# A narrower last block in the token-major input projection, and z's first rests moved ahead of a wait

## The chip, the core and the metric

The kernel runs on one core of a Trainium2 chip. The metric is the device time of the whole kernel in microseconds, median over runs; lower is better. The engines are TensorE (PE, with its weight loads PEld), VectorE (DVE), ScalarE (ACT), GpSimd (POOL) and SyncE (SP), which issues the DMAs of the weights.

## What is computed

Two transformer blocks over 256 tokens of width 1024 in f32. The first normalises x and multiplies it with `w_in`; the product is cut into the inputs of sparse attention (q, k, v, the indexer's iq, ik, iw), of a state-space branch (z, xbc, dt) and of the gates. Then come attention, the chunked scan, memory cross attention and a product-key expert layer. The second block is a gated linear recurrence with a convolutional feed-forward part, whose conditions enter by a modulation (`silu(c) @ w_ada`). What matters here is the beginning of the first block, in outline:

```python
IN_SPLIT_SIZES = (1024, 256, 256, 256, 64, 4, 2048, 3072, 32, 2048)  # q k v iq ik iw z xbc dt gate
y = (rmsnorm(x, norm_mix_g) @ w_in).split(IN_SPLIT_SIZES)
y = y * silu(z)                 # later, in the state-space branch
dt = softplus(dt_raw + dt_bias)
```

## The kernel before, in words

Nearly all matmuls are with weights that are streamed once from memory, in tiles of 128 x 1024 f32 (512 KB). SP loads them into `weight_ring`, a ring of four; a slot is loaded again when its tile's rest has been made. Every f32 product is made of three matmuls of the type fp32r: both operands are split into a high part and a rest, and high x high, rest x high and high x rest are accumulated in PSUM. For a weight tile e this goes through three engines, with two buffers each for the parts:

- ScalarE copies the tile to `weight_high` (`split_high`, line 1676 by the helper `func`), once the high matmuls of tile e - 2 are done and its rest is made. Semaphore `hi_ready`.
- VectorE or GpSimd subtracts: `weight_rest = tile - weight_high` (`split_rest`, line 2307 on VectorE, line 851 on GpSimd). It waits for `hi_ready` of the tile and for `hi_begun`, the first high matmul of the tile before. Semaphore `rest_ready`, one counter for both engines, so that the order of the tiles has to be kept.
- TensorE (`split_tile`, lines 964 to 972; matmuls at line 934) does the matmuls with the high part, then waits for `rest_ready` and does those with the rest.

The token-major projections (`split_block`, lines 974 to 999) keep 128 tokens as the stationary operand and stream 512 weight columns. A block is 512 output columns: four weight tiles, each with two chunks of 128 inputs, times two halves of the tokens, so eight high matmuls and four rest matmuls a tile, into two banks. There are four token-major blocks "tok" (tiles 0 to 15: q, k, iq, ik, v, iw, dt), and then four blocks "z" (tiles 16 to 31). The columns of "tok" are 1892, padded with zeros by the host to 2048: the last block holds columns 1536 to 2047, of which 356 carry values. ScalarE copies the banks of each "tok" block into `TOK` (`evacuate_tok`, lines 1761 to 1766), those of block 3 after the high parts of tiles 16 and 17. After that it makes the SiLU of the second block's conditions (`silu_of_conditions`, semaphore `silu_c`), for which it first loads an activation table.

Who makes the rests before the change: tiles 0 to 2 VectorE, 3 to 15 GpSimd (line 855), 16 to 31 VectorE (`z_rests`, line 2393), 32 on GpSimd. VectorE's queue around the change, by hand in this order (lines 2389 to 2425): wait for 16 rests; wait for `silu_c`; `group_sum`, a small reduction; rests of z's tiles 0 and 1; wait for the banks of "tok" and for the rope sines; then the rests of z's tiles 2 to 11 between the rope operations on `TOK` (lines 2415 to 2422); then tiles 12 to 15. Between the rests of z, `add_both` (lines 2370 to 2387) adds four tiles of the modulation's weights, scaled with the SiLU of the conditions, from the same ring; SP's queue waits for each of these sums in its turn, since it loads in the order of the ring.

After z, TensorE waits for `rope_ready` and transposes q, k, iq and ik, does the indexer's products, and then the gate (tiles 32 on, feature-major, 256 columns), the attention and the xbc projection with the convolution on VectorE.

Of the kernel before, what the change touches and what calls it, by code (L numbers as in the profile page):

```python
# [23 lines left out]
TT = T // P  # L24
# [118 lines left out]
for _name, _w in [("ident", P), ("upto", P), ("ones", P), ("after", P), ("before", P), ("causal", P),  # L143
                  ("iota", P), ("freq", 24), ("iota16", 16)]:
    CONST[_name] = (_c, _w)
    _c += _w
N_CONST = _c
N_LEVELS = 7
HALF_LEVELS = (range(0, 4), range(4, 7))
N_MADE = N_LEVELS + 1  # L150
# [305 lines left out]
def build(nc, A):  # L456
    B = plan_banks()
    with ExitStack() as ctx:
# [32 lines left out]
        x1_hi = over("x1_high", "arena", 30208, [P, KC, T])  # L491
        x1_lo = over("x1_rest", "act_feature_major", 0, [P, KC, T])
# [57 lines left out]
        S = {n: sem(n) for n in names}  # L550
# [46 lines left out]
        def claim(name, turn=None):  # L597
            b, n = B.at[name]
            if turn is not None:
                nc.tensor.wait_ge(bank_free[b], turn * B.per[name] + (n - 1))  # L600
            elif n > 1:
                nc.tensor.wait_ge(bank_free[b], n - 1)
            return ps[:, b, :]
# [19 lines left out]
        TOK = area(0, TT, 2048)  # L623
# [142 lines left out]
        tsl = lambda t: slice(t * P, (t + 1) * P)  # L766
# [77 lines left out]
        def _(pool):  # L844
# [7 lines left out]
                                        ALU.subtract).then_inc(S["rest_ready"], 1)  # L852

            pool.wait_ge(S["rest_ready"], 3)
            for e in range(3, 16):
                split_rest(e)
            pool.wait_ge(S["rest_ready"], 32)
            with pool.Fori(0, 2) as i:
# [73 lines left out]
        def _(pe):  # L932
            def mm(out, lhsT, rhs, start=True, stop=True):
                return nc.tensor.matmul(out, lhsT, rhs, start=start, stop=stop, skip_group_check=True)  # L934
# [36 lines left out]
                pe.wait_ge(rest_ready, rest_count)  # L971
                return rest(w_lo[:, e % 2, :])

            def split_block(e, name, b, hi, lo_, parts=None):

                banks = [claim((name, b, t)) for t in range(TT)]
                for j in range(4):
                    if parts is not None:
                        parts(j)

                    def high(w):
                        for t in range(TT):
                            for k in range(2):
                                r = w[:, k * 512:(k + 1) * 512]
                                ins = mm(banks[t], hi[:, 2 * j + k, tsl(t)], r, start=(j == k == 0), stop=False)
                                if t == k == 0:
                                    begun = ins
                                ins = mm(banks[t], lo_[:, 2 * j + k, tsl(t)], r, start=False, stop=False)
                        return begun, ins

                    def rest(w):
                        for t in range(TT):
                            for k in range(2):
                                ins = mm(banks[t], hi[:, 2 * j + k, tsl(t)], w[:, k * 512:(k + 1) * 512],
                                         start=False, stop=(j == 3 and k == 1))
                            if j == 3:
                                filled(ins, (name, b, t))

                    split_tile(e + j, None, 0, high, rest, *rest_count(e + j))
# [39 lines left out]
                    both_ready("x1", 2 + j)  # L1039

            for b in range(4):
                split_block(4 * b, "tok", b, x1_hi, x1_lo, x1_parts if b == 0 else None)
            for b in range(4):
                split_block(E0["in_z"] + 4 * b, "z", b, x1_hi, x1_lo)

# [9 lines left out]
            b = claim(("ad0", "sums"))  # L1055
            for c in range(2):
                for k in range(4):
                    ins = mm(b[:, 2 * k + c:2 * k + c + 1], ADS0[:, c, hsl(k)], C("ones")[:, 0:1])
# [3 lines left out]
            for t in range(TT):  # L1062
                for r in range(2):
                    b = claim(("idx", t, r))
                    rs = slice(r * IDH, (r + 1) * IDH)
                    for c in range(2):
                        ins = mm(b[:, c * T:(c + 1) * T], IQT[rs, c, tsl(t)], IKT[rs, :])
                    filled(ins, ("idx", t, r))
            with pe.Fori(0, 2) as i:
                for j in range(8):  # L1070
                    e = E0["in_gate"] + j
                    split_channels(e, ("gate", j), x1_hi, x1_lo, i, 8, S["rest_ready"], i * 8 + rest_count(e)[1])

            for t in range(TT):
                w = P * (t + 1)
                for p in range(4):
                    b = claim(("lg", t, p))
                    for c in range(2):
                        h = 2 * p + c
                        ins = mm(b[:, c * T:c * T + w], QT[:, h, tsl(t)], KT[:, h // 4, 0:w])  # L1080
# [3 lines left out]
            b = claim(("acs",))  # L1084
# [4 lines left out]
            for x in range(2):  # L1089
                ins = mm(b[64 * x:64 * x + 64, 128:256], ADT.rearrange("p c h -> p (c h)"), C("upto"))  # L1090
# [32 lines left out]
            for n in range(24):  # L1123
                e = E0["in_xbc"] + n
# [85 lines left out]
            for k in range(len(groups) + 1):  # L1210
                if k < len(groups):
                    c, g = groups[k]
                    for half in range(2):
                        b = claim(("row", c, g, half))
# [17 lines left out]
                if k >= 1:  # L1232
# [6 lines left out]
                    b = claim(("yd", c, g))  # L1239
                    for j in range(8):  # L1240
                        h = 8 * g + j
                        ins = mm(b[:, j * SP_:(j + 1) * SP_], EM[:, (k - 1) % 2, j, :],
                                 XS[:, c, h * SP_:(h + 1) * SP_])
                    filled(ins, ("yd", c, g))
                    if c == 0:
                        b = claim(("st", g))
                        filled(mm(b, BTOK[:, g, :], XDTD[:, g * 512:(g + 1) * 512]), ("st", g))
                    else:
                        freed(pe, ("st", g))
                        b = claim(("yo", g))  # L1250
# [3 lines left out]
            for n in range(8):  # L1254
                e = E0["mem_k"] + n
# [9 lines left out]
            for n in range(8):  # L1265
                e = E0["merge"] + 3 * n
# [15 lines left out]
            for n in range(8):  # L1282
                e = E0["cross_q"] + n
# [17 lines left out]
            for t in range(TT):  # L1301
                for p in range(2):
                    b = claim(("cl", t, p))
                    for c in range(2):
                        h = 2 * p + c
                        for k in range(2):
                            ins = mm(b[:, c * T:(c + 1) * T], CQT[:, 2 * h + k, tsl(t)], MKT[:, 2 * h + k, :],
                                     start=(k == 0), stop=(k == 1))
# [15 lines left out]
            for h in range(MH):  # L1324
                b = claim(("co", h))
                for c in range(2):
                    for m in range(TT):
                        ins = mm(b[:, c * T:(c + 1) * T], MV[:, m, h * MD + c * P:h * MD + (c + 1) * P],
                                 CPT[:, m, h, :], start=(m == 0), stop=(m == 1))
# [9 lines left out]
            for t in range(TT):  # L1339
                for h in range(2):  # L1340
                    b = claim(("y", t, h))
# [5 lines left out]
            with pe.Fori(0, 2) as i:  # L1347
                for j in range(8):
                    e = E0["peer_q"] + j
# [4 lines left out]
            for t in range(TT):  # L1354
                for q in range(4):
                    b = claim(("sk", t, q))
# [315 lines left out]
        def _(act):  # L1672
# [5 lines left out]
            def evacuate(job, out, turn=None, f=ACT.Copy, src=None, **kw):  # L1678
                b = arrived(act, job, turn)
                free(func(out, b if src is None else src(b), f, **kw), job)  # L1680
# [78 lines left out]
                    split_high(1)  # L1759

            def evacuate_tok(b):
                for t in range(TT):
                    evacuate(("tok", b, t), TOK[:, t, b * 512:(b + 1) * 512])
                if b == 0:
                    act.wait_ge(S["rope_arg"], 1)
                    func(ROPE.rearrange("p a b c -> p (a b c)"), ROPET[:, 4, :], ACT.Sin).then_inc(S["rope_sin"], 1)
# [498 lines left out]
        def _(dve):  # L2265
# [35 lines left out]
            def split_rest(e, ready, turn=None, n=8):  # L2301

                i_ = 0 if turn is None else turn
                dve.wait_ge(S["hi_ready"], i_ * n + (e + 1))
                if e > 1:
                    dve.wait_ge(S["hi_begun"], i_ * n + e)
                tt(w_lo[:, e % 2, :], raw(e)[0], w_hi[:, e % 2, :], ALU.subtract).then_inc(S[ready], 1)  # L2307
# [78 lines left out]
                else:  # L2386
                    signal(ins, "summed")

            dve.wait_ge(S["rest_ready"], 16)
            dve.wait_ge(S["silu_c"], 1)  # L2390
            step(V.tensor_reduce(group_sum[:, :], ident.rearrange("p (g c) -> p c g", g=4)[:, 0:2, :], AX.X, ALU.add))

            def z_rests(*tiles):
                for i in tiles:
                    split_rest(E0["in_z"] + i, "rest_ready")
                    if i in (3, 4, 6, 7, 9, 10, 12, 13):
                        add_both(12 + i // 3 - 1, i % 3, ADS0)

            z_rests(0, 1)
            for b in range(4):  # L2400
                for t in range(TT):
                    freed(dve, ("tok", b, t))
# [866 lines left out]
```

## Time and profile before

| what | us |
|---|---|
| median of 3 runs | 1806.13 |
| lowest and highest | 1805.28, 1807.16 |
| span of the profiled execution | 1795.7 |
| TensorE busy | 1744.2 |
| VectorE busy | 1251.2 |
| ScalarE busy | 942.1 |
| GpSimd busy | 492.9 |

The span runs from the first to the last instruction of the profiled execution. The profile gives no total of its own for that execution; the runs' median is 10.4 us above its span. Matmuls are pipelined: each is shown with its own duration, longer than the distance to the next, so the distance of their starts tells their rate. A few matmul records are missing.

### The profile page before, as it was taken

How to read it: one execution, taken by the hardware profiler on the slowest of the kernel's cores; microseconds unless marked ns; L12 is line 12 of the kernel's file. 1: busy time of each engine (PE TensorE's matmuls, PEld its weight loads, DVE VectorE, ACT ScalarE, POOL GpSimd, SP SyncE). 2: the span in 40 equal slices, each digit the busy share in tenths (PEclk: the TensorE clock that was granted, in tenths of full speed). 3: DMA queues.
4: the chain of work that ended last, by engine and by line, in shares of the span. 5: the costliest groups of instructions: out<-in, count | busy, mean ns of one | idle time of the engine just before them, and what ended most of it. 6: DMA issues, size and time to landing. Idle time of an engine off the chain costs nothing.

```text
span 1795.7 us, 33010 instructions
## 1 busy us (share of the span) xinstructions
PE 1744.2 (97%) x11190; PEld 1547.2 (86%) x11190; DVE 1251.2 (70%) x2359; ACT 942.1 (52%) x1389; POOL 492.9 (27%) x225
## 2 busy tenths in 40 slices
PE   9999989999999999999999999999999999999997
PEld 6799878897878999999999988888888787669996
DVE  4567587876424499067777578888888896667777
ACT  5466577544555544567777643333333575334444
POOL 4246744401568588800000000000000100013332
PEclk9999999999999999999999999999999999999999
DMA  6654443577344478755565687677767783355553
GB/s 216 200 188 141 166 152 118 190 248 266 121 164 150 135 222 228 228 179 172 174 173 173 195 263 239 235 235 236 237 239 236 272 276 122 113 176 187 183 183 113
DMA packets 122839, 347.63 MB, mean 194 GB/s; under 512 B 13904, under 2 KB 46800, under 8 KB 122512
## 3 DMA queue, kind: packets, MB, share of 16 engines
q1 hardware_dynamic: 121248, 339.52, 58.1%
q0 software_dynamic: 1520, 7.21, 1.1%
q8 instruction: 40, 0.66, 0.1%
q14 instruction: 31, 0.25, 0.0%
HBM read 328.84 MB, written 17.83 MB: 193 GB/s over the span
## 4 chain that ended last, share of the span: by engine, by line
PE 84%; DVE 6%; ACT 4%; issue 2%; POOL 2%; DMA 1%; POOLq 0%; DVEq 0%; ACTq 0%
PE banks L934 83%; POOL weight_rest L851 2%; ACT arena L1676 2%; DMA weight_ring<-in_stream 1%; ACT weight_high L1676 1%; PE banks L945 1%; DVE weight_rest L2307 1%; ACT span_exponentials L1676 0%; DVE arena L3110 0%; DVE arena L2991 0%; DVE arena L2348 0%; ACT scratch L1676 0%; ACT L1676 0%; DVE arena L2347 0%; DVE arena L2345 0%
## 5 line engine op out<-in xcount | busy, mean ns | idle before, releaser
L1676 ACT ACTIVATE weight_high<-weight_ring 128x1024 fp32r<-128x1024 f32 x448 | 473.0, 1057 | 453.4 <-PE banks L934 350.4
L851 POOL TENSOR_TENSOR weight_rest<-weight_ring,weight_high 128x1024 fp32r<-128x1024 f32 x165 | 414.4, 2521 | 264.5 <-ACT weight_high L1676 155.0
L2307 DVE TENSOR_TENSOR weight_rest<-weight_ring,weight_high 128x1024 fp32r<-128x1024 f32 x283 | 346.1, 1224 | 156.3 <-ACT weight_high L1676 153.4
L934 PE MATMUL banks<-a_high,weight_high 128*128 128x256 f32 x1216 | 304.0, 288 | 0.2 <-ACT weight_high L1676 0.2
L934 PE MATMUL banks<-a_rest,weight_high 128*128 128x256 f32 x1216 | 297.8, 283 | 0.0
L934 PEld LDWEIGHTS banks<-a_high,weight_high 128*128 128x128 f32 x1216 | 232.6, 191 | 1.5 <-issue 1.1
L934 PEld LDWEIGHTS banks<-a_rest,weight_high 128*128 128x128 f32 x1216 | 232.9, 192 | 0.3 <-issue 0.2
L934 PE MATMUL banks<-weight_high,gated_high 128*128 128x512 f32 x512 | 201.4, 393 | 0.0
L934 PE MATMUL banks<-weight_high,gated_rest 128*128 128x512 f32 x512 | 200.2, 391 | 0.0
L934 PE MATMUL banks<-a_high,weight_rest 128*128 128x256 f32 x1216 | 170.9, 283 | 2.4 <-POOL weight_rest L851 2.4
L934 PE MATMUL banks<-x_high,weight_high 128*128 128x256 f32 x672 | 167.5, 287 | 4.7 <-DVE x_rest L3079 3.7
L1676 ACT ACTIVATE arena<-banks 128x512 f32<-128x512 f32 (+4 forms) x219 | 145.2, 686 | 42.6 <-PE banks L934 37.9
L934 PE MATMUL banks<-x_rest,weight_high 128*128 128x256 f32 x672 | 166.1, 284 | 0.0
L934 PEld LDWEIGHTS banks<-a_high,weight_rest 128*128 128x128 f32 x1216 | 156.8, 192 | 3.2 <-POOL weight_rest L851 3.2
L934 PE MATMUL banks<-weight_rest,gated_high 128*128 128x512 f32 x512 | 140.5, 395 | 0.0
L934 PEld LDWEIGHTS banks<-x_high,weight_high 128*128 128x128 f32 x672 | 129.5, 193 | 7.1 <-ACT x_high L1676 3.9
L1676 ACT ACTIVATE small<-banks 128x256 f32<-128x256 f32 x128 | 48.9, 382 | 163.6 <-PE banks L934 163.5
L934 PEld LDWEIGHTS banks<-x_rest,weight_high 128*128 128x128 f32 x672 | 129.7, 193 | 1.3 <-issue 0.5
L934 PEld LDWEIGHTS banks<-weight_high,gated_high 128*128 128x128 f32 x512 | 96.0, 188 | 23.3
L934 PEld LDWEIGHTS banks<-weight_high,gated_rest 128*128 128x128 f32 x512 | 96.3, 188 | 21.8
L934 PEld LDWEIGHTS banks<-weight_rest,gated_high 128*128 128x128 f32 x512 | 96.3, 188 | 21.3
L3110 DVE SCALAR_TENSOR_TENSOR arena<-banks,cols,arena 128x189 f32<-128x189 f32 (+2 forms) x176 | 76.0, 432 | 46.4 <-ACT arena L1676 25.6
(360 smaller groups left out, 3101.5 us busy)
## 6 DMA issues: line engine op xcount, KB each, us to landing
weight_ring<-in_stream SPq DMA_DIRECT2D x512, 512.0 KB, 3.5
arena<-in_stream SPq DMA_DIRECT2D x66, 512.0 KB, 3.3
unit_spill<-small SPq DMA_DIRECT2D x128, 128.0 KB, 3.6
scratch<-unit_spill SPq DMA_DIRECT2D x128, 128.0 KB, 3.2
residual<-in_x SPq DMA_DIRECT2D x2, 512.0 KB, 4.1
arena<-in_mem POOLq DMA_DIRECT2D x2, 512.0 KB, 5.3
arena<-in_ctx POOLq DMA_DIRECT2D x2, 512.0 KB, 4.8
arena<-in_keys POOLq DMA_DIRECT2D x1, 1024.0 KB, 5.2
```

The costliest lines, as they stand in the source:

```text
L851: nc.gpsimd.tensor_tensor(w_lo[:, e % 2, :], raw(e)[0], w_hi[:, e % 2, :], ALU.subtract).then_inc(S["rest_ready"], 1)
L934: return nc.tensor.matmul(out, lhsT, rhs, start=start, stop=stop, skip_group_check=True)
L945: ins = nc.tensor.transpose(b[:, k * P:(k + 1) * P], src, ident)
L1676: return nc.scalar.activation(out, in_, f, **kw)
L2307: tt(w_lo[:, e % 2, :], raw(e)[0], w_hi[:, e % 2, :], ALU.subtract).then_inc(S[ready], 1)
L3110: ins = stt(o[:, ro, wo], x[:, ri, wi], tap(k), o[:, ro, wo], ALU.mult, ALU.add)
```

## The change

The last "tok" block is multiplied over its first 356 columns only (matmuls and the copies to `TOK`); the loads, high parts and rests of its tiles stay 1024 wide. The rests of its four tiles, 12 to 15, go from GpSimd's queue to VectorE's, ahead of `group_sum`, and VectorE's wait is for 12 rests instead of 16. The wait for `silu_c` moves behind the rests of z's tiles 0 and 1.

```diff
--- before.py
+++ after.py
@@ -145,6 +145,7 @@
     CONST[_name] = (_c, _w)
     _c += _w
 N_CONST = _c
+TOK_USED = 1892
 N_LEVELS = 7
 HALF_LEVELS = (range(0, 4), range(4, 7))
 N_MADE = N_LEVELS + 1
@@ -852,7 +853,7 @@
                                         ALU.subtract).then_inc(S["rest_ready"], 1)
 
             pool.wait_ge(S["rest_ready"], 3)
-            for e in range(3, 16):
+            for e in range(3, 12):
                 split_rest(e)
             pool.wait_ge(S["rest_ready"], 32)
             with pool.Fori(0, 2) as i:
@@ -971,9 +972,9 @@
                 pe.wait_ge(rest_ready, rest_count)
                 return rest(w_lo[:, e % 2, :])
 
-            def split_block(e, name, b, hi, lo_, parts=None):
-
-                banks = [claim((name, b, t)) for t in range(TT)]
+            def split_block(e, name, b, hi, lo_, parts=None, width=512):
+
+                banks = [claim((name, b, t))[:, 0:width] for t in range(TT)]
                 for j in range(4):
                     if parts is not None:
                         parts(j)
@@ -981,7 +982,7 @@
                     def high(w):
                         for t in range(TT):
                             for k in range(2):
-                                r = w[:, k * 512:(k + 1) * 512]
+                                r = w[:, k * 512:k * 512 + width]
                                 ins = mm(banks[t], hi[:, 2 * j + k, tsl(t)], r, start=(j == k == 0), stop=False)
                                 if t == k == 0:
                                     begun = ins
@@ -991,7 +992,7 @@
                     def rest(w):
                         for t in range(TT):
                             for k in range(2):
-                                ins = mm(banks[t], hi[:, 2 * j + k, tsl(t)], w[:, k * 512:(k + 1) * 512],
+                                ins = mm(banks[t], hi[:, 2 * j + k, tsl(t)], w[:, k * 512:k * 512 + width],
                                          start=False, stop=(j == 3 and k == 1))
                             if j == 3:
                                 filled(ins, (name, b, t))
@@ -1039,7 +1040,7 @@
                     both_ready("x1", 2 + j)
 
             for b in range(4):
-                split_block(4 * b, "tok", b, x1_hi, x1_lo, x1_parts if b == 0 else None)
+                split_block(4 * b, "tok", b, x1_hi, x1_lo, x1_parts if b == 0 else None, min(512, TOK_USED - 512 * b))
             for b in range(4):
                 split_block(E0["in_z"] + 4 * b, "z", b, x1_hi, x1_lo)
 
@@ -1759,8 +1760,9 @@
                     split_high(1)
 
             def evacuate_tok(b):
-                for t in range(TT):
-                    evacuate(("tok", b, t), TOK[:, t, b * 512:(b + 1) * 512])
+                width = min(512, TOK_USED - 512 * b)
+                for t in range(TT):
+                    evacuate(("tok", b, t), TOK[:, t, b * 512:b * 512 + width], src=lambda bank_: bank_[:, 0:width])
                 if b == 0:
                     act.wait_ge(S["rope_arg"], 1)
                     func(ROPE.rearrange("p a b c -> p (a b c)"), ROPET[:, 4, :], ACT.Sin).then_inc(S["rope_sin"], 1)
@@ -2386,8 +2388,9 @@
                 else:
                     signal(ins, "summed")
 
-            dve.wait_ge(S["rest_ready"], 16)
-            dve.wait_ge(S["silu_c"], 1)
+            dve.wait_ge(S["rest_ready"], 12)
+            for e in range(12, 16):
+                split_rest(e, "rest_ready")
             step(V.tensor_reduce(group_sum[:, :], ident.rearrange("p (g c) -> p c g", g=4)[:, 0:2, :], AX.X, ALU.add))
 
             def z_rests(*tiles):
@@ -2397,6 +2400,7 @@
                         add_both(12 + i // 3 - 1, i % 3, ADS0)
 
             z_rests(0, 1)
+            dve.wait_ge(S["silu_c"], 1)
             for b in range(4):
                 for t in range(TT):
                     freed(dve, ("tok", b, t))
```

## Rows read from the trace of the kernel before

**Rows 1.** The page: the span, and busy time, share and instructions by engine.

```profile
span 1795.7 us, 33010 instructions
PE 1744.2 (97%) x11190; PEld 1547.2 (86%) x11190; DVE 1251.2 (70%) x2359; ACT 942.1 (52%) x1389; POOL 492.9 (27%) x225
```

**Rows 2.** Stretches: length, busy time (count) of PE, PEld, DVE, ACT, POOL; clock, DMA, GB/s.

```profile
46.67:57.55 10.88, 10.88 (x49) 9.01 (x48) 0.00 (x0) 5.21 (x7) 7.43 (x4) 1.00 0.58 194
57.55:63.06 5.51, 3.00 (x13) 2.18 (x12) 2.47 (x3) 3.84 (x6) 0.00 (x0) 1.00 0.05 19
63.06:103.88 40.82, 40.82 (x181) 33.74 (x180) 32.86 (x60) 18.43 (x22) 2.12 (x1) 1.00 0.73 251
120.00:150.00 30.00, 30.00 (x252) 30.00 (x252) 27.88 (x42) 17.60 (x24) 26.62 (x12) 1.00 0.58 193
```

**Rows 3.** TensorE in order of time: start, length, what, idle before and its releaser.

```profile
57.55 0.39 PE L934 MATMUL banks<-weight_high,x_high 128*128 128x512 f32 x1
...
62.03 1.19 PE L934 MATMUL banks<-weight_rest,x_high 128*128 128x512 f32 x4 [2.50 <-DVE weight_rest L2307]
63.06 0.40 PE L934 MATMUL banks<-weight_high,x_high 128*128 128x512 f32 x1
```

**Rows 4.** The chain that ended last, in order of time: start, length, what.

```profile
58.94 1.28 ACT L1676
...
60.24 0.22 ACT silu_of_conditions L1676
...
60.55 0.18 DVE group_sum L2391
...
60.76 1.24 DVE weight_rest L2307
...
192.54 1.56 DVE arena L2485 x4
```

**Rows 5.** GpSimd in order of time, tiles 11 and 12.

```profile
41.77 2.40 POOL L851 TENSOR_TENSOR weight_rest<-weight_ring,weight_high 128x1024 fp32r<-128x1024 f32 x1 [0.32 <-ACT weight_high L1676]
44.49 2.40 POOL L851 TENSOR_TENSOR weight_rest<-weight_ring,weight_high 128x1024 fp32r<-128x1024 f32 x1 [0.32 <-ACT weight_high L1676]
```

**Rows 6.** ScalarE in order of time, 46 to 95 us.

```profile
46.98 1.06 ACT L1676 ACTIVATE arena<-banks 128x512 f32<-128x512 f32 x2
...
54.18 1.06 ACT L1676 ACTIVATE weight_high<-weight_ring 128x1024 fp32r<-128x1024 f32 x1 [1.66 <-PE banks L934]
56.90 1.06 ACT L1676 ACTIVATE weight_high<-weight_ring 128x1024 fp32r<-128x1024 f32 x1 [1.66 <-PE banks L934]
...
76.49 1.06 ACT L1676 ACTIVATE weight_high<-weight_ring 128x1024 fp32r<-128x1024 f32 x1 [2.13 <-DMA weight_ring<-in_stream]
...
93.47 1.06 ACT L1676 ACTIVATE weight_high<-weight_ring 128x1024 fp32r<-128x1024 f32 x1 [2.79 <-DMA weight_ring<-in_stream]
```

**Rows 7.** VectorE in order of time: the rests of z's tiles 2 to 6.

```profile
63.60 1.23 DVE L2307 TENSOR_TENSOR weight_rest<-weight_ring,weight_high 128x1024 fp32r<-128x1024 f32 x1 [0.48 <-PE banks L934]
...
66.52 1.23 DVE L2307 TENSOR_TENSOR weight_rest<-weight_ring,weight_high 128x1024 fp32r<-128x1024 f32 x1
...
69.04 1.23 DVE L2307 TENSOR_TENSOR weight_rest<-weight_ring,weight_high 128x1024 fp32r<-128x1024 f32 x1 [0.50 <-ACT weight_high L1676]
...
71.73 1.22 DVE L2307 TENSOR_TENSOR weight_rest<-weight_ring,weight_high 128x1024 fp32r<-128x1024 f32 x1
...
74.48 1.23 DVE L2307 TENSOR_TENSOR weight_rest<-weight_ring,weight_high 128x1024 fp32r<-128x1024 f32 x1 [0.35 <-ACT weight_high L1676]
```

**Rows 8.** VectorE in order of time: two operations of one shape in the indexer.

```profile
115.51 0.29 DVE L2443 TENSOR_TENSOR arena<-arena,const 128x128 f32<-128x128 f32 x1
...
121.58 2.41 DVE L2448 TENSOR_TENSOR arena<-arena 128x128 f32<-128x128 f32 x1
```

**Rows 9.** TensorE in order of time: the plain f32 matmuls at the kernel's start.

```profile
1.47 7.10 PE L934 MATMUL banks<-arena 128*128 128x512 f32 x10 [1.47 <-DVE arena L2309]
```

**Rows 10.** TensorE's weight loads in order of time: one load.

```profile
57.56 0.19 PEld L934 LDWEIGHTS banks<-weight_high,x_rest 128*128 128x128 f32 x1
```

## The prediction

> **What bounds the kernel now.** I read the page first: TensorE (PE) is busy for 97% of the span [rows 1], so a change shows in the end only where it shortens TensorE's matmuls or a gap between them; work taken off the other engines is free of value. Next the table of stretches [rows 2]. The last token-major block (46.67 to 57.55 us) is 10.88 us of TensorE without a gap, while VectorE is busy for 0.00 us. The following 5.51 us, from the first matmul of z's tile 0 to the first of tile 1, have TensorE busy for 3.00 only. The rest of the z block, 40.82 us, is again all TensorE. All four stretches have the granted clock at 1.00, so no clock term enters.
>
> Then TensorE in order of time [rows 3] and the chain of waits [rows 4] around the gap. A tile of a block takes 10.88 / 4 = 2.72 us: twelve matmuls of 512 columns, eight with the high part of the weights and four with their rest, each starting 10.88 / 48 = 0.2267 us after the one before. The ninth of z's tile 0, the first that needs its rest, could start at 57.55 + 8 x 0.2267 = 59.36, and it starts at 62.03. The chain says why: ScalarE's table load (58.94), the SiLU of the conditions (60.24), VectorE's group_sum (60.55), VectorE's rest of z's tile 0 (60.76), and only then TensorE. The rest itself needs nothing of the SiLU; it stands behind `dve.wait_ge(S["silu_c"], 1)` in VectorE's queue. z's tile 0 lasts 63.06 - 57.55 = 5.51 instead of 2.72: **the wait costs 2.79 us**. These two places are what the change touches.
>
> **Part 1, the narrower block.** Per tile twelve matmuls go from 512 to 356 columns; four tiles make 48. No row has a width of 356. The nearest on both sides are 512 columns at 0.2267 us start to start, and the gate's matmuls of 256 columns, 252 in 30.00 us [rows 2], 0.119 each. The slope is (0.2267 - 0.119) / 256 = 0.42 ns a column, so 356 columns should take 0.2267 - 156 x 0.00042 = 0.161 us. The bounds: no better than the 256 row (0.108 saved, 5.2 us in all), no worse than the 512 row (0); a slower rate is a rival below. I take the line, since 356 lies between and two widths at one clock fix it: 48 x 0.0656 = **3.1 us**. A tile now takes 1.93 us.
>
> The row contradicts one rule. The Trainium skill (TensorE: Matmul & The Clock Gate, Back-to-back issue gap) gives a sustained spacing of about 81 ns for 128 columns and 131 ns for 512, which is 0.13 ns a column. By that the block would give back an estimated 48 x 156 x 0.13 ns = 1.0 us.
>
> Can the feeders keep a 1.93 us tile? GpSimd's rest takes 2.40 us [rows 5] and could not; four of them would set 2.40 or more per tile. The change gives tiles 12 to 15 to VectorE, whose rest takes 1.22 to 1.24 [rows 4, 7] and which does nothing there [rows 2]. Its new wait, for twelve rests, ends when GpSimd's rest of tile 11 does; that piece lies one tile ahead of the 44.49 one, at 41.77 to 44.17, before VectorE could begin tile 12 in any case (44.49). Behind that wait is nothing that was not behind the wait for sixteen. ScalarE's high part needs 1.06 us a tile and waits for the eight high matmuls two tiles back: tile 16's began at 54.18, 8 x 0.2267 + 0.25 us after tile 14 (52.11), tile 17's at 56.90 [rows 6]; now tile 17's begins at T15 + 8 x 0.161 + 0.2 = 53.9. Putting the tiles at T12 = 46.67 (the start of the stretch) and then T13 = 48.60, T14 = 50.53, T15 = 52.46, T16 = 54.39, the tightest is tile 14: ScalarE has also the two copies of block 2, 46.98 to 48.04 [rows 6], then 1.06, ready at 49.2 and wanted at 50.53. No stall. The loads come earlier, since VectorE releases a ring slot 1.2 us sooner than GpSimd did. The two narrower copies of block 3 save a tenth or two on ScalarE, costed at nothing.
>
> **Part 2, z's first rests ahead of the wait.** Tiles are numbered on: 16 is z's tile 0. Its high part is ready near 53.1, VectorE's group_sum (0.18) is past, its rest ends at about 54.4, and TensorE wants it at 54.39 + 1.81 = 56.20: the gap is gone. Tile 17's high part runs 53.9 to 55.0, its rest 55.0 to 56.3, wanted at 57.11 + 1.81. The whole 2.79 us are gained if nothing else is late.
>
> What is late next? ScalarE: from the start of tile 17's high part (56.90) to the end of the SiLU (60.45) it took 3.55 us [rows 4, 6]; now 53.9 + 3.55 = 57.5. Tile 18's high part then ends at 58.6 and TensorE wants it at T18 = 59.83: margin 1.2. VectorE waits for the SiLU until 57.5 and does z's tile 2 at 58.6 to 59.9, wanted at 61.6. Behind it come the rope operations; by the spacings of [rows 7] (63.60 to 66.52, then 2.02 of work to 69.04 less its 0.50 idle, 2.69, 2.40) the rests of tiles 19 to 22 start at 61.5, 63.6, 66.3 and 68.7, and end 1.5, 2.2, 2.3 and 2.7 us before TensorE wants them. VectorE stands about 1.0 us later against TensorE than before at tile 19, and the idle times of [rows 7] take that up by tile 22 or 23. One more follows: the load of z's tile 7 waits in SP's queue behind the one that needs the first condition tile summed, which now happens 0.5 us later against TensorE. ScalarE got that tile at 76.49 after 2.13 idle for the load [rows 6], ended it at 77.55 and TensorE wanted it at 63.06 + 6 x 2.72 = 79.4; the margin falls from 1.85 to about 1.3. The tightest load, at 93.47, belongs to z's tile 13, wanted at 63.06 + 12 x 2.72 = 95.7: margin 95.7 - 94.53 = 1.2, and it lies after VectorE has caught up. Covered, all of it; if one cover went, its price is its excess over the margin, under 1 us.
>
> **The sum.** 3.15 + 2.79 = 5.9 us. From the end of z on, transposes, gate, attention and all later stages start from semaphores of what lies before, so all queues move up together. The page gives the profiled execution's span, 1795.7, and no total of its own; the median of the runs is 1806.13, 10.4 above. That stays, so span 1789.8 and time 1806.1 - 5.9 = **1800.2**.
>
> **Rivals.**
> (a) *Only part of the stall goes*: tile 18's high part or VectorE's rests in z come late. For it: the margins are 1.2 and 1.5 us and VectorE is busy 32.86 of 40.82 us there [rows 2]. Against: to lose 1 us they must be wrong by over 2. Time 1801 to 1802. Chance 0.07.
> (b) *Narrow matmuls give little*, since the weight load ahead of each, 0.19 us [rows 10], sets the spacing: 48 x (0.2267 - 0.19) = 1.8 us saved instead of 3.1, 1801.5; with nothing saved 1803.3. Against it are the 256 rows: the same loads, and a matmul each 0.119 us, so loads overlap more than this. Chance 0.05.
> (c) *The gain is given back later* by a changed meeting of VectorE and GpSimd. A 128x128 tensor-tensor took 0.29 us at 115.51 and 2.41 at 121.58 [rows 8], where GpSimd is in its rests for 26.62 of 30.00 us [rows 2]: about 2.1 us for one unlucky meeting. In the convolutions after 164 us such VectorE work is in the chain that sets the end [rows 4]. One or two such losses leave 3.8 or 1.7 us of gain: 1802.3 to 1804.4. Against: engines shift together, and three runs with their own DMA jitter lie within 1.9 us. Chance 0.12. The Trainium skill (SBUF — State Buffer, SBUF: two separate sides) has the pair of ports as an exclusive lock held for a whole instruction; the rows agree, 2.41 against the 2.40 of GpSimd's rest [rows 5].
> (d) *Slower*: the 48 matmuls of 356 columns fall to the rate of plain f32 matmuls. The ten plain ones of 512 columns took 7.10 us [rows 9], 0.71 each; at 356 columns 0.49, so 48 x (0.49 - 0.227) = +12.8, less 2.8: +10 us, 1816. It decides from a spacing of 0.2267 + 2.8 / 48 = 0.285 us on. Against: 256 and 512 columns of the same type lie on one line. Chance 0.03.
> That the change doesn't do what it says is excluded for the wait, which is plain in the queue; for the width it is (b).
>
> **The numbers.** The forecast has 0.73. Its own range is 1799.3 to 1801.1, from the spacing (0.155 to 0.166) and a median's scatter. The range to hold 8 in 10 takes in (a), most of (b) and a first loss of (c): 1798.4 to 1803.3; the low end allows a spacing of 0.150 and a sample low by 1 us. About 0.2%, 3.6 us, is what a measurement can tell from none. Faster by more: 0.73 + 0.07 + half of (b) + a third of (c), 0.86; within: 0.11; slower: 0.03.
>
> **What the profile after would show.** Tiles 12 to 15 at 1.93 us each, starts 0.161 apart; four VectorE rests of 1.22 from about 44.5 on and GpSimd idle until the gate; z's tile 0 beginning near 54.4, its ninth matmul 0.227 after the eighth, the next tile near 57.1; the SiLU ending near 57.4 with VectorE idle for about 1 us before z's tile 2; the transposes after z at 97.9 instead of 103.9. Wrong would be: tiles of 2.1 us or more (width or feeders), a TensorE wait at tile 18 or at z's tile 3 or 7 (the stall has moved), or the 6 us present at 98 us and absent at the end (case c).

## The result, and the profile after

| | median us | lowest to highest | runs |
|---|---|---|---|
| before | 1805.7 | 1802.56 to 1807.16 | 6 |
| after | 1795.3 | 1792.97 to 1798.5 | 6 |

The ratio is 0.9949, 95% interval 0.9935 to 0.9962: 6.9 to 11.7 us faster. The forecast was 5.9 us and 1800.2 us, with a range of 1798.4 to 1803.3. The sign was right, the size too small, and the time lies below the range. On two later occasions the same pair gave 0.9946 (0.9931 to 0.9961) and 0.9964 (0.9951 to 0.9977).

The page of the changed kernel; its profiled execution took 1796.22 us in all:

```profile
span 1794.4 us, 33010 instructions
PE 1744.4 (97%) x11190; PEld 1548.5 (86%) x11190; DVE 1258.4 (70%) x2363; ACT 942.1 (53%) x1389; POOL 482.9 (27%) x221
```

The span is only 1.3 us shorter than in [rows 1], and TensorE is busy as long as before. So the spans of two executions can't tell what the change is worth here; further traces, below, show where they part. I go first to the place of the change. The stretches of the changed kernel (columns as in [rows 2]): the narrow block, z's tile 0, the rest of z.

```profile
46.86:54.54 7.68, 7.68 (x49) 7.67 (x48) 4.92 (x5) 4.94 (x7) 0.00 (x0) 1.00 0.76 236
54.54:57.26 2.72, 2.72 (x14) 2.26 (x13) 1.29 (x2) 2.69 (x5) 0.00 (x0) 1.00 0.81 276
57.26:98.08 40.82, 40.82 (x182) 33.74 (x181) 32.73 (x59) 19.50 (x23) 2.16 (x1) 1.00 0.69 243
```

And TensorE in order of time:

```profile
46.86 0.32 PE L935 MATMUL banks<-weight_high,x_high 128*128 128x356 f32 x1
47.02 0.32 PE L935 MATMUL banks<-weight_high,x_rest 128*128 128x356 f32 x1
...
54.54 0.39 PE L935 MATMUL banks<-weight_high,x_high 128*128 128x512 f32 x1
...
56.35 1.07 PE L935 MATMUL banks<-weight_rest,x_high 128*128 128x512 f32 x4
57.26 0.39 PE L935 MATMUL banks<-weight_high,x_high 128*128 128x512 f32 x1
```

The first two lines show the distance of two starts, 47.02 - 46.86 = 0.16 us. The block takes 7.68 us instead of 10.88: 48 matmuls at 0.160 us, 3.20 us saved. z's tile 0 takes 2.72 instead of 5.51: 2.79 saved. The rest of z takes 40.82 us in both [rows 2], so nothing was given back there. VectorE, in order of time, shows the margins:

```profile
44.67 1.23 DVE L2309 TENSOR_TENSOR weight_rest<-weight_ring,weight_high 128x1024 fp32r<-128x1024 f32 x1 [16.28 <-ACT weight_high L1677]
...
53.38 1.23 DVE L2309 TENSOR_TENSOR weight_rest<-weight_ring,weight_high 128x1024 fp32r<-128x1024 f32 x1 [0.67 <-ACT weight_high L1677]
55.24 1.23 DVE L2309 TENSOR_TENSOR weight_rest<-weight_ring,weight_high 128x1024 fp32r<-128x1024 f32 x1 [0.64 <-ACT weight_high L1677]
58.63 1.23 DVE L2309 TENSOR_TENSOR weight_rest<-weight_ring,weight_high 128x1024 fp32r<-128x1024 f32 x1 [2.16 <-ACT weight_high L1677]
...
61.55 1.23 DVE L2309 TENSOR_TENSOR weight_rest<-weight_ring,weight_high 128x1024 fp32r<-128x1024 f32 x1
...
68.67 1.23 DVE L2309 TENSOR_TENSOR weight_rest<-weight_ring,weight_high 128x1024 fp32r<-128x1024 f32 x1 [0.20 <-ACT weight_high L1677]
```

z's tiles 0 and 1 get their rests at 53.38 and 55.24, ahead of the SiLU, which ends at 57.45 (ScalarE below); tiles 2, 3 and 6 at 58.63, 61.55 and 68.67, against 58.6, 61.5 and 68.7 in the forecast. At tile 6 VectorE waits again (0.20 us) and has caught up. ScalarE in order of time (the lines at 70.97 and 87.70 are z's tiles 7 and 13):

```profile
57.23 0.22 ACT L1677 ACTIVATE silu_of_conditions<-cols 128x16 f32<-128x16 f32 x1
57.36 1.05 ACT L1677 ACTIVATE weight_high<-weight_ring 128x1024 fp32r<-128x1024 f32 x1
...
70.97 1.06 ACT L1677 ACTIVATE weight_high<-weight_ring 128x1024 fp32r<-128x1024 f32 x1 [2.42 <-DMA weight_ring<-in_stream]
...
87.70 1.06 ACT L1677 ACTIVATE weight_high<-weight_ring 128x1024 fp32r<-128x1024 f32 x1 [2.84 <-DMA weight_ring<-in_stream]
```

Their high parts end at 72.03 and 88.76 and TensorE wants them at about 73.6 and 89.9, so neither load became late. The chain that ended last, in order of time, first of the changed kernel:

```profile
32.18 66.05 PE banks L935 x304
98.23 2.84 PE banks L946 x26
...
113.07 16.94 PE banks L935 x139
```

then of the kernel before:

```profile
104.04 2.84 PE banks L945 x26
...
118.88 51.68 PE banks L934 x418
```

From 32.18 on the chain stays on TensorE until z is done: TensorE waits for nothing. The transposes start at 98.23 instead of 104.04, and the gate's third tile gets its rest matmuls at 113.07 instead of 118.88: 5.81 us both times. That is 3.20 + 2.79 = 5.99, less the 0.19 us by which this execution comes to the narrow block later (46.86 against 46.67). The local forecast holds in every term. What is left to explain is why single spans differ by 1.3 us and medians by 10.

One column had not been followed past 104 us: the granted clock. The changed kernel in stretches:

```profile
240.00:250.00 10.00, 7.49 (x52) 5.46 (x52) 5.40 (x12) 7.93 (x18) 1.39 (x1) 0.83 0.52 193
250.00:260.00 10.00, 7.99 (x53) 5.95 (x53) 9.16 (x15) 9.10 (x24) 0.00 (x0) 0.93 0.30 111
260.00:270.00 10.00, 10.00 (x52) 7.47 (x51) 6.72 (x11) 5.63 (x18) 0.00 (x0) 0.73 0.00 0
...
1490.00:1500.00 10.00, 10.00 (x71) 9.75 (x70) 4.08 (x6) 3.83 (x10) 0.00 (x0) 0.83 0.20 60
```

and the kernel before in the same ones:

```profile
240.00:250.00 10.00, 7.86 (x64) 7.42 (x62) 6.72 (x18) 7.93 (x13) 6.32 (x3) 1.00 0.64 211
250.00:260.00 10.00, 9.38 (x70) 6.67 (x71) 7.10 (x11) 9.79 (x26) 0.00 (x0) 1.00 0.59 211
260.00:270.00 10.00, 6.87 (x36) 5.11 (x35) 8.99 (x13) 6.13 (x17) 0.00 (x0) 0.83 0.00 0
...
1490.00:1500.00 10.00, 10.00 (x77) 9.38 (x76) 5.67 (x7) 4.18 (x10) 0.00 (x0) 1.00 0.38 112
```

Between 240 and 270 us TensorE waits in part of the time. In 1490 to 1500 it is busy for all 10 us, at a mean of 0.83 of full clock after and 1.00 before. Over the whole span the mean clock was 0.992 after and 0.994 before.

### The profile page after: what moved, and what is told of

Same layout as the page of the kernel before. It is cut to its first block, busy times and chain, and to the rows that moved or that the text cites. A ratio compares the mean times of both kernels' runs of the same rounds, so it can differ in the third digit from the quotient of the medians.

```text
span 1794.4 us, 33010 instructions
## 1 busy us (share of the span) xinstructions
PE 1744.4 (97%) x11190; PEld 1548.5 (86%) x11190; DVE 1258.4 (70%) x2363; ACT 942.1 (53%) x1389; POOL 482.9 (27%) x221
## 4 chain that ended last, share of the span: by engine, by line
PE 84%; DVE 6%; ACT 4%; POOL 2%; issue 2%; DMA 1%; POOLq 0%; DVEq 0%; SPq 0%; ACTq 0%
PE banks L935 83%; POOL weight_rest L852 2%; ACT arena L1677 2%; DMA weight_ring<-in_stream 1%; ACT weight_high L1677 1%; PE banks L946 1%; DVE weight_rest L2309 1%; DVE ssd_rest L2335 1%; ACT span_exponentials L1677 0%; DVE arena L3114 0%; DVE attention_rest L2597 0%; ACT scratch L1677 0%; DVE arena L2995 0%; DMA residual<-in_x 0%; DVE arena L2350 0%
## 5 line engine op out<-in xcount | busy, mean ns | idle before, releaser
L852 POOL TENSOR_TENSOR weight_rest<-weight_ring,weight_high 128x1024 fp32r<-128x1024 f32 x161 | 404.8, 2523 | 270.4 <-ACT weight_high L1677 158.6
L2309 DVE TENSOR_TENSOR weight_rest<-weight_ring,weight_high 128x1024 fp32r<-128x1024 f32 x287 | 351.1, 1224 | 180.0 <-ACT weight_high L1677 177.1
```

The source lines that it names most:

```text
L852: nc.gpsimd.tensor_tensor(w_lo[:, e % 2, :], raw(e)[0], w_hi[:, e % 2, :], ALU.subtract).then_inc(S["rest_ready"], 1)
```

## The experiments

The experiments test two theories. **A**: the change is worth its local 5.8 us; the rest is TensorE's clock, granted at half rate (1.2 instead of 2.4 GHz) in different places from one execution to the next, the removed gap among them. **B**: something further down gains another 3 us each time. Means are given with their standard error, against the kernel before on the same occasion. The diffs show the changed lines alone.

**n_before**: the kernel before, no edit.

> The kernel before, unchanged, against itself. Both theories: 0 in the mean. Theory A (the change is worth its local 5.8 us and the rest of the measured gain lies in where TensorE's clock is granted at half rate): single runs spread over 4 to 6 us, and the slower ones show a lower mean granted clock (0.988 to 0.994). Theory B (the change gives 9 us by something that is systematic further down): no such relation is needed, and the profiled execution has its stages where the profile of before has them, within 0.5 us.

Mean 1803.21 us over 12 runs, 0.0 +- 0.9 against before. Single runs reach from 1797.75, at a mean clock of 0.995, to 1806.89 at 0.989. Over all runs, each kernel with a mean of its own, a fit gives about 1.2 us for each 0.001 of mean clock. That covers about 60% of the variance within a kernel. So the time goes with the clock, as A says, but not all of the 9 us of spread does.

**p_width**: the narrow block and VectorE's rests alone (the diff is against the changed kernel).

```diff
             for e in range(12, 16):
                 split_rest(e, "rest_ready")
+            dve.wait_ge(S["silu_c"], 1)
...
             z_rests(0, 1)
-            dve.wait_ge(S["silu_c"], 1)
```

> Narrow last block and the rests of tiles 12 to 15 on VectorE; the wait for the SiLU back ahead of z's first rests. In the trace, by both theories: tiles 12 to 15 at 1.92 us, and the gap at z's tile 0 stays 2.8 us or a little less, so the transposes after z start 3.1 us earlier than before. Time: A: 3.1 us less, give or take 2 for the clock. B: 3.1 us, or up to 6.5 us less if the extra gain comes with the narrow block.

Ratio 0.9985 (0.9972 to 0.9998); means differ by 2.9 +- 0.9 us, as counted. In its trace the transposes after z start at 102.66, only 1.4 us earlier than in the profile of before and not the 3.1 expected. TensorE in order of time shows why:

```profile
59.27 2.07 PE L935 MATMUL banks<-weight_rest,x_high 128*128 128x512 f32 x4 [2.45 <-DVE weight_rest L2309]
61.14 0.63 PE L935 MATMUL banks<-weight_high,x_high 128*128 128x512 f32 x1
...
61.99 0.53 PE L935 MATMUL banks<-weight_high,x_high 128*128 128x512 f32 x1
62.37 0.40 PE L935 MATMUL banks<-weight_high,x_rest 128*128 128x512 f32 x1
```

After the gap, four rest matmuls take 61.14 - 59.27 = 1.87 us; in [rows 3] the same four took 1.03. The next three (61.14, 61.57 and 61.99) are shown with 0.63 or 0.53 us instead of 0.39. Full rate is back at 62.37. The granted clock is 0.50 from 59 to 62 us and 1.00 from 62.3 on. So here the gap is followed by a stretch at half clock, and in the profile of before it is not.

**p_wait**: the moved wait alone (the diff is against the kernel before).

```diff
             dve.wait_ge(S["rest_ready"], 16)
-            dve.wait_ge(S["silu_c"], 1)
...
             z_rests(0, 1)
+            dve.wait_ge(S["silu_c"], 1)
```

> The wait for the SiLU behind z's first two rests; block of 512 columns and GpSimd's rests as before. In the trace, by both theories: no gap at z's tile 0, transposes after z 2.8 us earlier. Time: A: 2.8 us less, give or take 2. B: 2.8, or up to 6 us less if the extra gain comes with the wait.

Ratio 0.9970 (0.9959 to 0.9981), means 4.9 +- 0.8 us apart, while the transposes after z start at 101.39 instead of 104.04, 2.65 us earlier. So on this occasion an extra gain of 2.2 +- 0.8 us comes with the wait, and none with the width.

**n_after**: the changed kernel, no edit.

> The changed kernel, unchanged, on another occasion. A: 5.8 us less than before in the mean, between 4 and 9, and another profile of it shows other places of half clock. B: 9 us less again, within 1 us.

8.4 +- 1.2 us; ratio above. That lies inside what A allowed (4 to 9) and inside B's 9 within 1, so this run doesn't part them. The profiled execution was the longest of the six, 1799.88 us at a clock of 0.990, the shortest 1792.29 at 0.995.

**w_fill**: the kernel before, its gap filled with matmuls whose result nobody reads (`keep_busy`); `claim` waits until a PSUM bank is free.

```diff
                 done.then_inc(S["hi_used"], 1)
+                if turn is None and e == E0["in_z"]:
+                    claim(("z", 1, 1))
+                    keep_busy(5)
                 pe.wait_ge(rest_ready, rest_count)
```

> The kernel before, with five plain matmuls of 512 columns whose result nobody reads put into TensorE's gap at z's tile 0 (2.1 us of work in a gap of 2.5). The wait for the SiLU and its 2.8 us stay. Theory A (what the change gives beyond its local 5.8 us comes from the clock, which in part of the executions is granted at half rate right behind that gap, as in the profile of the width-only kernel at 59 to 62 us): the time falls by 1 to 2 us against before though no wait is removed. Theory B (the extra comes from elsewhere): the same as before, within 0.5 us, or up to 0.3 slower where the dummies run over.

The means are equal, 0.3 +- 0.7 us less than before. But the dummies ran longer than I had counted:

```profile
59.44 4.45 PE L934 MATMUL banks<-arena 128*128 128x512 f32 x10
63.33 1.50 PE L934 MATMUL banks<-weight_rest,x_high 128*128 128x512 f32 x4
64.66 0.39 PE L934 MATMUL banks<-weight_high,x_high 128*128 128x512 f32 x1
```

A plain f32 matmul shows as two records: five of them, 10 records, take 3.9 us to the next start, in a gap of 2.5. z's tile 1 starts at 64.66 instead of 63.06, so TensorE's sequence is 1.6 us longer and the time isn't. Something is given back, 1.9 +- 0.7 us, but only by this sum; that it is the clock behind the gap, as A has it, is not shown by this run.

**w_fill2**: the same with `keep_busy(2)`, which fits into the gap.

> The kernel before with only two dummies in the gap: 1.7 us of work in 2.5 us, so TensorE's own sequence is not lengthened and the wait for the SiLU stays. Theory A (half clock behind the gap in part of the executions): nothing moves in the trace and the time still falls, by 1 to 2 us in the mean. Theory B: no difference, within 0.5 us.

0.6 +- 0.8 us less than before, ratio 0.9998 (0.9987 to 1.0009), where A expected 1 to 2. It points in the direction of A and can't be told from nothing. This test, meant as the clean one, is inconclusive.

**n_before2, b3, b4**: the kernel before in further executions.

> The kernel before once more, for another profiled execution and more runs with their clocks. Theory A: where this execution is slower than 1797.5 us, its trace has more stretches at half clock than the profile of before, one of them perhaps behind the gap at 59 us, and the difference is their cost. Theory B: it is slower at the same clock, in some stage that can be named.

> The kernel before, one profiled execution more. A: if it takes over 1802 us, its trace shows more half clock than the profile of before, likely behind the gap at 59 us (1.4 us) and at 260, 415 and 1500 us. B: over 1802 us at the same number of such stretches.

> The kernel before, another execution with a trace; theories A and B expect the same as of the last one: more half clock where it is slow (A), or the same number of stretches and a slower stage (B).

n_before2 took 1800.94 us in its profiled execution (12 runs: mean 1802.1). It has no half clock at the gap. Its span of 1799.1 is 3.4 us above that of the profile of before at the same mean clock, 0.994, which is what B expected of it; where they part is shown below. b3 took 1804.35 and b4 1803.21, and both have it. Stretches of b3, then b4, then the profile of before:

```profile
60.00:70.00 10.00, 7.71 (x27) 6.18 (x28) 7.14 (x13) 3.07 (x5) 0.00 (x0) 0.83 0.49 158
```

```profile
60.00:70.00 10.00, 7.62 (x26) 6.12 (x27) 7.07 (x13) 3.10 (x5) 0.00 (x0) 0.83 0.47 158
```

```profile
60.00:70.00 10.00, 7.96 (x35) 6.62 (x36) 8.32 (x14) 3.63 (x5) 0.00 (x0) 1.00 0.61 185
```

and TensorE in b3 in order of time:

```profile
62.29 1.98 PE L934 MATMUL banks<-weight_rest,x_high 128*128 128x512 f32 x4 [2.50 <-DVE weight_rest L2307]
64.07 0.63 PE L934 MATMUL banks<-weight_high,x_high 128*128 128x512 f32 x1
64.50 0.63 PE L934 MATMUL banks<-weight_high,x_rest 128*128 128x512 f32 x1
...
66.75 1.09 PE L934 MATMUL banks<-weight_rest,x_high 128*128 128x512 f32 x4
67.68 0.39 PE L934 MATMUL banks<-weight_high,x_high 128*128 128x512 f32 x1
```

From the end of the gap to z's tile 2 b3 takes 67.68 - 62.29 = 5.39 us. At full clock it would be 1.03 + 2.72 = 3.75, as [rows 3] and the 2.72 us of a tile have it. **The half clock behind the gap costs 1.6 us**. Of the six traced executions with the open gap (before, n_before, n_before2, b3, b4, p_width) three have it; of the six traced without the gap (after, n_after, n_after2, p_wait, p_pool, s_sin) and the two with it filled none has. If the gap had nothing to do with it, three such executions among fourteen would all fall on these six in one case of 18. So A's mechanism and its price are shown; how often it occurs is not well known. On the frequency of three in six it is worth about 0.8 us in the mean.

The traces also show where executions part behind z. These are the starts of five of ScalarE's activation table loads, one place of the program in each column (us):

| execution | place 1 | place 2 | place 3 | place 4 | place 5 |
|---|---|---|---|---|---|
| before | 250.77 | 305.86 | 1398.15 | 1501.51 | 1780.22 |
| n_before2 | 251.01 | 306.11 | 1398.41 | 1505.19 | 1783.66 |
| b3 | 252.68 | 312.53 | 1405.24 | 1508.51 | 1787.09 |
| after | 244.98 | 301.61 | 1394.23 | 1500.73 | 1778.95 |
| n_after | 244.90 | 304.79 | 1397.36 | 1504.32 | 1782.57 |
| n_after2 | 244.84 | 304.10 | 1396.64 | 1502.50 | 1780.92 |

From place 2 to place 3 all six take 1092.3 to 1092.7 us, so B's gain is not there. From place 1 to place 2 they take 55.1 to 59.9, longer where more of it is at half clock: the mean clock from 240 to 300 us is 0.97 in before (55.1) and 0.91 in after (56.6). From place 3 to place 4 they take 103.3 to 107.0, and there the amount of half clock doesn't decide: before and after both have a mean clock of 0.98 from 1400 to 1500 us. TensorE waits there for ScalarE's high parts for 2.8 us in before, 4.3 in after and 5.2 in n_before2, and the half clock falls on another place. What makes these waits vary is open. In neither stage is a traced execution of the changed kernel ahead of the best of before.

**n_after2**: the changed kernel, once more.

> The changed kernel once more. A and B: 7.5 to 9 us less than before in the mean; its fastest execution 5.5 to 6 us below the fastest of before, which is the local gain without the clock's part.

6.1 +- 0.9 us; the fastest, 1794.18, is 3.4 below the fastest of before, not 5.5 to 6. Over all occasions the changed kernel's 18 runs have a mean of 1795.4, and 95 runs of before taken with the experiments 1802.7: 7.2 +- 0.6 us. Their mean clocks are 0.9919 and 0.9920, with an error of 0.0003, so the mean clock doesn't show the 1.4 us beyond the local 5.8; by the fit above that would be 0.0012.

**p_pool**: the changed kernel, rests of tiles 12 to 15 back on GpSimd.

```diff
-            for e in range(3, 12):
+            for e in range(3, 16):
...
-            dve.wait_ge(S["rest_ready"], 12)
-            for e in range(12, 16):
-                split_rest(e, "rest_ready")
+            dve.wait_ge(S["rest_ready"], 16)
```

> The changed kernel with the rests of tiles 12 to 15 back on GpSimd. As forecast: a rest takes 2.40 us plus some 0.1 to 0.3 to the next, so the narrow tiles are paced by GpSimd at 2.4 to 2.6 us instead of 1.92 once the lead is used up; of the narrow block's 3.1 us 1 to 2 remain, and the kernel is 1 to 2 us slower than the changed one. Rival: the lead of one tile covers it and it equals the changed kernel.

GpSimd, then TensorE, in order of time:

```profile
47.48 7.12 POOL L852 TENSOR_TENSOR weight_rest<-weight_ring,weight_high 128x1024 fp32r<-128x1024 f32 x3 [0.26 <-ACT weight_high L1677]
```

```profile
47.00 0.32 PE L935 MATMUL banks<-weight_high,x_high 128*128 128x356 f32 x1
...
54.65 0.92 PE L935 MATMUL banks<-weight_rest,x_high 128*128 128x356 f32 x4 [0.15 <-POOL weight_rest L852]
55.40 0.39 PE L935 MATMUL banks<-weight_high,x_high 128*128 128x512 f32 x1
```

GpSimd's last three rests run back to back, 2.37 each, against tiles of 1.92, as forecast. But its lead covers all except the end: two short delays, at tiles 14 and 15. The block takes 55.40 - 47.00 = 8.40 us instead of 7.68. The mean is 6.3 +- 0.9 us below before, which can't be told from the changed kernel. Moving the rests was worth 0.7 us in the trace, not one to two.

**s_sin**: the changed kernel, with the rope sine one block later.

```diff
-                if b == 0:
+                if b == 1:
                     act.wait_ge(S["rope_arg"], 1)
```

> The changed kernel with ScalarE's rope sine (and its table load) one block later, so that the high parts of tiles 5 and 6 don't stand behind VectorE's angle chain. In the profile before TensorE waits 1.0 us at 29.56 for the high part and another 0.5 us for GpSimd's rest after it. Expected by the same way of counting: 1.5 to 2 us less than the changed kernel, z's end at 96.3 instead of 98.2. Rival: the copies of block 1 then stand in front of a high part and the wait comes back there: no gain.

In the kernel before TensorE waits twice here:

```profile
29.56 0.50 PE L934 MATMUL banks<-weight_high,x_high 128*128 128x512 f32 x1 [1.01 <-ACT weight_high L1676]
...
32.04 1.20 PE L934 MATMUL banks<-weight_rest,x_high 128*128 128x512 f32 x4 [0.37 <-POOL weight_rest L851]
```

With the edit neither wait is left; the chain of s_sin:

```profile
19.86 76.37 PE banks L935 x351
96.23 2.84 PE banks L946 x26
```

The transposes start 2.00 us before those of the changed kernel. ScalarE in order of time shows why the rival failed:

```profile
33.32 1.06 ACT L1677 ACTIVATE weight_high<-weight_ring 128x1024 fp32r<-128x1024 f32 x1 [1.66 <-PE banks L935]
...
35.37 1.28 ACT L1677 ACT_TABLE_LOAD   x1
37.22 0.28 ACT L1677 ACTIVATE arena<-arena 128x96 f32<-128x96 f32 x1 [0.57 <-DVE arena L2367]
37.41 1.04 ACT L1677 ACTIVATE weight_high<-weight_ring 128x1024 fp32r<-128x1024 f32 x1
```

By the pace of the tiles the next high part was due at 33.32 + 2.72 = 36.04; it comes at 37.41, 1.4 us late, and ScalarE's lead covers it. The six runs have a median of 1792.28 us (1790.9 to 1793.89), ratio 0.9945 (0.9933 to 0.9958), means 10.0 +- 0.6 us below before. It is the best of the kernels run, about 3 us below the mean of the changed one over all occasions; 1.5 to 2 were expected.

## Why the prediction was right, and where it was wrong

- **Part 1, the narrower block**: right. 0.160 us a matmul against 0.161 forecast, 3.20 us against 3.15. The line between the 256 and the 512 rows held, with 0.43 ns a column from 356 to 512. The estimate of 1.0 us that the prediction sets beside it is refuted by the 3.20.
- **The feeders**: right that VectorE keeps pace. The step that GpSimd "would set 2.40 or more per tile" left out its lead: in p_pool only the end of the block is delayed, by 0.7 us.
- **Part 2, the moved wait**: the gap is gone and 2.79 us with it, next waits and margins as worked out. No load and no rest became late. One sign was worked out wrongly: VectorE idle "for about 1 us" before z's tile 2, where the prediction's own times give 2.3 (56.3 to 58.6); it was 2.16.
- **From the end of z on "all queues move up together"**: right as far as the traces can show it. The 5.8 us are there until 250 us. Behind that, two stages shift single executions by several us, in before as in after.
- **What failed in the gain** is the sentence "All four stretches have the granted clock at 1.00, so no clock term enters". It read one execution. In half of the traced executions with the gap the clock falls to half right behind it, 1.6 us. The price of the wait was 2.79 plus a clock term, 1.6 where it occurs and about 0.8 in the mean, and only the first was counted. p_wait measured 2.2 +- 0.8 us beyond the local count, so the clock term may not be all of it.
- **The level failed too**: "the median of the runs is 1806.13, 10.4 above. That stays". Later runs of the same kernel have a mean of 1802.7. Of the 4.8 us by which the changed kernel's mean of 1795.4 lies under the forecast, 3.4 come from there and the rest from the gain. In the first measurement alone before had 1805.7, so there the miss is nearly all gain, 10.4 us instead of 5.9; the later occasions have 8.4 and 6.1, so part of the 10.4 was chance. The range allowed 1 us for such scatter, where single runs spread by 9. I also took the 10.4 us between span and median for a constant outside the profiled execution. In the profiled runs with both numbers it is 1.8 us (1796.22 against 1794.4); the remaining 8.6 were a quick execution compared with three long ones.
- **Rivals**: (a) and (b) did not occur. (c), a later meeting of VectorE and GpSimd that takes the gain back: its sign, 6 us present at 98 us and absent at the end, is there in the profile of after, 1.3 us at the end. But the 5.8 us stand unchanged through the indexer and the convolutions up to 250 us, and 3.1 us of the loss fall between 1398 and 1502, where n_before2 loses 3.4 without any edit. (d) is excluded by the 0.160 us.

Open stays how the extra is shared out. The mechanism shown gives 0.8 us in the mean, the local gain 5.8, together 6.6; the difference over all occasions is 7.2 +- 0.6, the first measurement's interval 6.9 to 11.7. The rest may be chance. So A's mechanism is real, and with it the count of 6.6 lies within the error of the 7.2; a systematic gain further down, B, is seen in no trace. That half clock or waits at 250 to 306 and 1398 to 1502 us became fewer is not shown: the three traces of the changed kernel have no less of them, and the mean clock over all runs is the same.

## What to carry to other kernels

Price a gap on TensorE with what may follow it: ask whether the clock fell behind it in any traced execution, and look at more than one, since a profile with 1.00 throughout a stretch shows only that it can stay up. Compare the profiled execution's span with the spans of the timed runs before using their medians as a base; the difference of 10 us here was not overhead, it showed that the profile had caught a quick execution. When a wait is taken out at the head of a queue, a list of "ready at, wanted at" for the next five instructions gives the local gain; here it was right to 0.1 us.

## What was unexpected of the hardware

- The kernel's time spreads over 9 us (1797.6 to 1806.9) in executions that do the same work, at mean clocks of 0.995 to 0.989. Two of them with the same 0.994 still differ by 3.4 us of span.
- A gap of 2.5 us on TensorE is followed by half clock in some executions and not in others, with the same instructions: matmuls of 512 columns then start each 0.43 us instead of 0.227.
- A plain f32 matmul of 512 columns occupies TensorE for 0.78 us (five in 3.9 us) and is shown as two records. The row of warm-up matmuls [rows 9] counts records, so rival (d) took for a whole matmul what was half of one. At the start of the kernel the same five take 7.10 us, 1.42 each; why, no run tests.
